# Where the FFN norms' outputs begin in SBUF, relative to the weight tiles, modulo 256 bytes

## The chip, the cores and the metric

The kernel runs on one core of a Trainium2 chip. The metric is the device time of one execution in microseconds (us); lower is better. The times shown are medians over runs of the same program.

## What is computed

Two networks in a row over 256 tokens of width 1024, all in fp32. The first has two layers of FFN, three mixers side by side (SSD, mLSTM, RWKV) and a second FFN; the second takes 256 more context tokens in and has two layers of modulated FFN, a mixer (Fourier, then retention) and another FFN. What matters here are the eight FFNs:

```python
def swiglu(x, w_gate_up, w_down):
    gate, up = jnp.split(x @ w_gate_up, 2, axis=-1)
    return (jax.nn.silu(gate) * up) @ w_down
x = x + FFN_HALF * swiglu(rms_norm(x, ffn1_norm[l]), ffn1_w_gate_up[l], ffn1_w_down[l])   # width 1024 -> 2816 -> 1024
```

In the second network the norm's output is also scaled and shifted by a modulation vector, and the result is gated.

## The kernel before

**Precision.** Every large product of `a` and `b` is made of three fp32r matmuls: `a` is split into `hi` (a cast to fp32r) and `lo` (the rest), `b` likewise, and `mm3` issues hi x hi, hi x lo and lo x hi. All of them go through `mm` on line 102. ScalarE casts a weight tile (`split_hi`, L314), VectorE subtracts (`split_lo`, L320). `mm(p, o, l, r)` loads `l` into the array (stationary) and streams `r` (moving):

```python
def mm3(p, o, wh, wl, xh, xl, start, stop):
    mm(p, o, wh, xh, start, False)
    mm(p, o, wh, xl, False, False)
    return mm(p, o, wl, xh, False, stop)
```

**Stages and tiles.** The FFN stages are f10, f20, f11, f21 (first network) and half00, half02, half10, half12 (second). Five of them work on 256 tokens (the f stages and half12: narrow), three on 512 (half00, half02, half10: wide). The gate half of a stage (`Ffn.tensor`) has 22 weight tiles of 128 x 2048. Each makes 128 gate and 128 up columns: 2 x 8 x 3 = 48 matmuls, with weights stationary and the norm's output `hs` moving, 256 or 512 columns of it. That is 22 x 48 = 1056 matmuls a stage. The back half turns it round: `hf` (the SwiGLU result) is stationary, the down-projection's weights are moving, 512 columns at a time; in a narrow stage a tile is 24 matmuls, and there are 11. The mixers project in the gate half's way (`project_t`: weights stationary, `hx` moving, 256 columns, 48 matmuls a tile).

**Order.** `network` writes the order of the stages' phases out by hand; `plan` gives each weight tile one of up to eight raw buffers (`raw0` to `raw7`, and `lo` in the same place) and a slot for its `hi` part. Narrow FFN stages have three such slots, `hi0`, `hi1`, `hi2`, in turn; wide stages, and the mixers but for their first tile, have two. The first tile of a wide stage has a spare of its own. In the order of the plan `hi2` falls on 4 of the 11 back tiles of f10 and on 3 of 11 in each other narrow stage.

**Addresses.** `Map` hands out byte offsets within a partition. `raw`, `lo`, `hi0` and `hi1` all begin at 128 modulo 256 (the allocation starts at 4224), and so do `K.free` and `END`. I call that residue the class. Slices of these tiles step by 512 or 1024 bytes, so every slice keeps its tile's residue. Before the change, `STEP = 64`: the narrow stages' `hs`, `xs`, `no` and (f stages) `rot` begin 64 bytes past the class, and so does `hi2`. `hf` is in the class everywhere, `hs` of the wide stages too, and the mixers' `hx` too. `K.free` is where the stages' scratch area starts; `hi2` is its first 8192 bytes when three slots are used.

**The norm.** `Norm` writes `hs` in two parts: ScalarE the fp32r cast, VectorE the rest of it (`low`, L601). The first tile's matmuls wait for it chunk by chunk (`Norm.ready`).

Of the kernel before, what the change touches and what calls it, by code (L numbers as in the profile page):

```python
# [8 lines left out]
F32R = mybir.dt.float32r  # L9
# [12 lines left out]
ROWS = 27648  # L22
END = 229248
LINE = 128
STEP = 64
ALL = slice(None)


class Line:


    def __init__(self, sem):
        self.sem, self.n, self.at, self.counting = sem, 0, {}, True
# [120 lines left out]
class Core:  # L154


    def __init__(self, nc, A, ctx):
        self.nc, self.A, self.ctx = nc, A, ctx
        self.lines, self.stages, self.order, self.opening = {}, {}, [], {}
        m = Map(nc, (nc.sbuf_base + LINE - 1) // LINE * LINE)  # L160
        at = [m.at + 8192 * i for i in range(5)] + [END - 8192 * (2 + i) for i in range(RAW - 5)]
        m.at = at[4] + 8192
        self.raw = [Map(nc, at[i]).take(f"raw{i}", 2048) for i in range(RAW)]
        self.far = at[3]
        self.lo = [Map(nc, at[i]).take(f"lo{i}", 2048, dt=F32R) for i in range(RAW)]
        self.hi = [m.take(f"hi{i}", 2048, dt=F32R) for i in range(2)]
        self.xt = m.take("xt", 2, 1024)
        self.msk = m.take("msk", len(MASKS), 128)
        self.mask2 = m.take("mask2", 2, 128)
        self.scanm = m.take("scanm", 256)  # L170
        self.cols = m.take("cols", NCOLS)
        self.rows = m.take("rows", 120)
        self.mods = m.take("mods", 2, 72, 2)
        self.gcol = m.take("gcol", 3, 2, 8)
        self.growt = m.take("grow", 128)
        self.st = m.take("st", 512)
        self.silb = m.take("silb", 2, 1024)
        self.prod = m.take("prod", 1024)
        m.at = (m.at + LINE) // 256 * 256 + LINE
        self.free, self.end = m.at, END  # L180
        self.hi.append(Map(nc, m.at + STEP).take("hi2", 2048, dt=F32R))
        self.ps = [ctx.enter_context(nc.psum_tensor(f"ps{i}", [P, 512], F32)) for i in range(8)]
        (self.ident, self.tri, self.ones, self.negT, self.neg, self.bones, self.l2,
         self.l2t) = (self.msk[:, i, :] for i in range(8))
        self.lvl = [self.msk[:, 8 + i, :] for i in range(5)]
        self.i2 = self.msk[:, 13, 0:64]
        self.onesrow = self.msk[0:1, 2, :]
        c2 = 2 * NCOL1
        self.ng2 = self.cols[:, c2:c2 + 48].rearrange("p (l j c) -> p l j c", l=2, j=3)
        self.ab2 = self.cols[:, c2 + 48:c2 + 192].rearrange("p (l c) -> p l c", l=2)  # L190
        self.heads = self.cols[:, c2 + 192:c2 + 224].rearrange("p (c h) -> p c h", h=8)
        self.sct = self.st[:, 256:272].rearrange("p (c v) -> p c v", v=2)
        self.xa = [self.xt[:, t, :] for t in range(2)]
        self.ring = [Loads(self.sem(f"ring{i}")) for i in range(RAW)]
        self.wac, self.wdv = Part(self.line("w", "hi"), 0), Part(self.line("w", "lo"), 0)
# [495 lines left out]
class Half:  # L691


    gates = None
# [2197 lines left out]
def network(K):  # L2892

    A, order, stages = K.A, K.order, K.stages
    filled, rows_of = [0], []

    def put(name, stage):
        stages[name], stage.key = stage, name
        return stage
# [48 lines left out]

    def first(l, which, before, since=()):
        name, gain = f"f{which}{l}", "n1" if which == 1 else "n2"  # L2950
        norm = put(name + "n", Norm(K, name + "n", [before], K.xa, K.split(8192 + STEP, name + "hs", 8, 256),
                                    K.at(ROWS + STEP, name + "xs", 2, 1024), K.at(ROWS + 8192 + STEP, name + "no", 3, 512),
                                    lambda c, s: K.col(l, gain, c)))
        s = put(name, Ffn(K, name, norm, Half(K.xa), A[f"ffn{which}_w_gate_up"][l], A[f"ffn{which}_w_down"][l], [22], 2,
                          K.at(8192 + 16384 + STEP, name + "rot", 3, 256), K.split(ROWS + 16384, name + "hf", 22, 256)))
        s.since = since
        norm.idle = None if before is setup else (0, 15) if which == 1 else (4, 15)
        if before is setup:
            for _ in range(3):
                run(norm)  # L2960
            run(setup)
        else:
            join(before, norm)
        if (l, which) != (1, 2):
            ffn(s)
        return s
# [75 lines left out]
    def half_ffn(l, j, nt, parts, rows, before, xs, o, hs, gb, rot, fin, hf, spare, turn=None):  # L3042

        name, N = f"half{l}{j}", 128 * nt
        gb = K.at(gb, name + "gb", nt // 2, 1024)
        hs = [Map(K.nc, K.free + at).take(f"{name}hs{i}", 8, N, dt=F32R) for i, at in enumerate(hs)]
        hf = [Map(K.nc, K.free + at).take(f"{name}hf{i}", max(parts), N, dt=F32R) for i, at in enumerate(hf)]
        norm = put(name + "n", Norm(K, name + "n", [before], rows[:nt], hs, K.at(xs, name + "xs", nt, 1024),
                                    K.at(o, name + "no", 3, 512), lambda c, v: K.sct[:, c, v:v + 1],
                                    lambda c, v: K.mods[:, l, 24 * j + c, v:v + 1], (l, j), turn))  # L3050
        if j == 0:
            rows_of.append(put(f"grow{l}", GateRows(K, l, norm, 6)))
        gates = put(name + "g", Gates(K, name + "g", [norm], rows_of[l], j, nt // 2, gb))
        s = put(name, Ffn(K, name, norm, Gated(gates, rows, K.at(fin, name + "fin", 2, 512)), A["ffn_gu_2"][l, j // 2],
                          A["ffn_w_down_2"][l, j // 2], parts, nt, K.at(rot, name + "rot", 3, N), hf))
        if spare:
            s.spare = Map(K.nc, K.free + spare).take(name + "hi", 2048, dt=F32R)
        return norm, [rows_of[l]] * (0 if j else 2) + [gates], s
# [6 lines left out]
    both = K.xa + [ct[:, t, :] for t in range(2)]  # L3065
    s = setup
    for l in range(2):
        s = first(l, 1, s)
        s = first(l, 2, *mixers(l, s))

    rows1 = put("rows1", RowNorm(K, "rows1", [s], K.at(89088, "fn", 1024), K.at(ROWS, "junk1", 2, 1024), A["final_norm"],
                                 None, ct))
    s.loads = [rows1]
    norm, gates, half = half_ffn(0, 0, 4, [11, 11], both, rows1, ROWS, ROWS + 16384, (0, 72704), 16384, 93184, 89088,
                                 (ROWS, 50176), 16384, [2, 3, 0, 1])
    norm.idle = 0, 30
    ffn(s, [norm, norm], late=8)
    fill_to(36)
# [3 lines left out]
    gb, rot = K.at(49152, "four_gb", 2, 1024), K.at(59392, "four_fin", 2, 512)  # L3082
    gates = put("fourgates", Gates(K, "fourg", [half], rows_of[0], 1, 2, gb))
    four = put("four", Fourier(K, "four", half, 0, both, Gated(gates, both, rot)))
    for s in (half, half, four, half, half, four, gates, four, four, four, four, four, four):
        run(s)
    for _ in range(3):
        run(four)

    norm, gates, half = half_ffn(0, 2, 4, [11, 11], both, four, 0, 16384, (45056, 61440), 90112, 77824, 83968, (0, 22528),  # L3090
                                 90112)
    norm.idle = 0, 17
    join(four, norm)
# [2 lines left out]
    before = half  # L3096
    norm, gates, half = half_ffn(1, 0, 4, [11, 11], both, before, 45056, 61440, (0, 16384), 90112, 32768, 38912,
                                 (45056, 67584), 69632)
# [4 lines left out]
    yT, hs = K.at(8192, "retyT", 16, 256), K.split(24576, "reths", 8, 512)  # L3103
    m = Map(K.nc, K.free + 57344)
    norm = put("retn", Norm(K, "retn", [half], both, hs, K.at(8192, "retxs", 4, 1024), K.at(57344, "retno", 3, 512),
                            lambda c, v: K.sct[:, c, v:v + 1], lambda c, v: K.mods[:, 1, 24 + c, v:v + 1], (1, 1)))
# [4 lines left out]
    gb, rot = K.at(57344, "retgb", 1, 1024), K.at(63488, "retfin", 2, 512)  # L3111
    gates = put("retgates", Gates(K, "retg", [ret], rows_of[1], 1, 1, gb))
    rout = put("retout", Out(K, "retout", [ret], A["ret_w_out_2"][0], yT, ys, Gated(gates, K.xa, rot), 6))
# [4 lines left out]
    for q in range(rout.phases - rout.tail):  # L3118
        run(rout)
        if q < 1:  # L3120
            run(gates)

    norm, gates, half = half_ffn(1, 2, 2, [22], K.xa, rout, 8192 + STEP, 16384 + STEP, (53504 + STEP, 61696 + STEP), 69952,
                                 79872, 75776, (8192 + 256, 30720 + 256),
                                 None)
    half.since = [ret]
    norm.idle = 0, 21
    join(rout, norm)
    ffn(half, gates)
    K.final = put("rows2", RowNorm(K, "rows2", [half], K.at(83968, "fg", 1024), K.at(53504, "junk2", 2, 1024), A["final_g_2"],  # L3130
                                   K.out))
    half.loads = [K.final]
    for _ in range(half.tail):
# [167 lines left out]
```

How the kernel before makes its waits and increments, by code:

```python
    def wait_ge(self, sem, n):  # L84
        if n > self.seen.get(sem.name, 0):
            self.seen[sem.name] = n
            if not self.counting:
                self.eng.wait_ge(sem, n)
# [1 line left out]
    def __call__(self):  # L90
        if self.chained and self.before:
            self.wait_ge(*self.before)
        return self.eng
# [213 lines left out]
    def split_hi(self, a, w):  # L307
        s, n, r, width, _ = self.weights[w]
        before = self.hislot[w][1]
        a.wait_ge(*self.landed(r))
        if before is not None:
            a.wait_ge(*self.released(*self.weights[before][0:2]))
        a().activation(self.high(w), self.raw[self.place(r)][:, 0:width], ACT.Copy).then_inc(*a.mark(self.wac, w))
# [1 line left out]
    def split_lo(self, v, w):  # L316
        s, n, r, width, _ = self.weights[w]
        v.wait_ge(*self.wac[w])
        v().tensor_tensor(self.low(w), self.raw[self.place(r)][:, 0:width], self.high(w).bitcast(F32),
                          ALU.subtract).then_inc(*v.mark(self.wdv, w))
# [1 line left out]
    def fetch(self, sp):  # L323
        for src, width, s, _, i, _, before in self.tiles:
            if i >= s.near:
                s.opened(sp)
            if before is not None:
                sp.wait_ge(*self.released(*self.tiles[before][2:4]))
            dst = self.raw[i][:, 0:width]
            if len(src.shape) == 3:
                dst = dst.rearrange("p (c n) -> p c n", n=src.shape[2])
            sp().dma_start(dst, src, max_dma_last_dim=16384).then_inc(*self.ring[i].mark())
# [70 lines left out]
    def row(self, e, t, h):  # L404
        e.wait_ge(*self.x.all)
```

## Time and profile before

| | |
|---|---|
| median of 3 runs | 3314.3 us (3309.09 to 3314.7) |
| profiled execution, its own time | 3311.61 us |
| its span, first to last instruction | 3309.7 us |
| mean granted TensorE clock | 0.989 |
| TensorE busy | 3196.1 us (97%), 19162 matmuls |
| VectorE / ScalarE / GpSimd busy | 2015.0 / 1302.9 / 115.9 us |
| DMA moved | 469.30 MB, mean 142 GB/s |

The span is what the sums are made against; 1.9 us lie around it. A line of a group gives the engine, the operation, output and inputs by name (buffer numbers left out, so `hi` stands for all three slots), the shape, the count, and the mean duration of one. Durations of matmuls overlap. A line of the timeline begins with the start of an instruction, or of the first of several.

### The profile page before, as it was taken

How to read it: one execution, taken by the hardware profiler on the slowest of the kernel's cores; microseconds unless marked ns; L12 is line 12 of the kernel's file. 1: busy time of each engine (PE TensorE's matmuls, PEld its weight loads, DVE VectorE, ACT ScalarE, POOL GpSimd, SP SyncE). 2: the span in 40 equal slices, each digit the busy share in tenths (PEclk: the TensorE clock that was granted, in tenths of full speed). 3: DMA queues.
4: the chain of work that ended last, by engine and by line, in shares of the span. 5: the costliest groups of instructions: out<-in, count | busy, mean ns of one | idle time of the engine just before them, and what ended most of it. 6: DMA issues, size and time to landing. Idle time of an engine off the chain costs nothing.

```text
span 3309.7 us, 46055 instructions
## 1 busy us (share of the span) xinstructions
PE 3196.1 (97%) x19162; PEld 2792.5 (84%) x19162; DVE 2015.0 (61%) x2437; ACT 1302.9 (39%) x1566; POOL 115.9 (4%) x126
## 2 busy tenths in 40 slices
PE   7998999999999899999999999999999999999998
PEld 7988887898989888798888877888888888887897
DVE  5777557778786657678765745744343334444554
ACT  5444244544445234554422233222242233434443
POOL 0001200000000210000000000000000000000000
PEclk9999999999999999999999999999999999999999
DMA  6652021466663012457454521543222222332552
GB/s 237 241 208 77 28 100 64 191 242 229 255 240 111 28 63 76 172 212 282 161 179 140 186 98 51 198 139 102 96 98 87 102 96 77 124 102 102 197 188 93
DMA packets 84970, 469.30 MB, mean 142 GB/s; under 512 B 7717, under 2 KB 11525, under 8 KB 44058
## 3 DMA queue, kind: packets, MB, share of 16 engines
q1 hardware_dynamic: 77952, 451.44, 37.3%
q10 hardware_dynamic: 6810, 14.91, 1.3%
q8 instruction: 151, 2.47, 0.3%
q14 instruction: 57, 0.47, 0.0%
HBM read 465.23 MB, written 1.10 MB: 141 GB/s over the span
## 4 chain that ended last, share of the span: by engine, by line
PE 77%; DVE 14%; ACT 5%; issue 1%; DMA 1%; POOL 0%; DVEq 0%; ACTq 0%; SPq 0%; POOLq 0%
PE ps L102 76%; DVE lo L320 4%; ACT hi L314 2%; DVE prod L464 1%; PE ps L522 1%; DMA raw<-in_ffn_w_gate_up 0%; DVE m1restMs L1973 0%; DVE m0restMs L1973 0%; DVE xt L685 0%; DVE ct L685 0%; DMA raw<-in_ffn_gu 0%; DVE half00fin L683 0%; DMA raw<-in_ffn_w_down 0%; DVE f21rot L855 0%; ACT f21hf_h L833 0%
## 5 line engine op out<-in xcount | busy, mean ns | idle before, releaser
L320 DVE TENSOR_TENSOR lo<-raw,hi 128x2048 fp32r<-128x2048 f32 (+1 forms) x357 | 809.6, 2268 | 604.4 <-ACT hi L314 588.9
L314 ACT ACTIVATE hi<-raw 128x2048 fp32r<-128x2048 f32 (+1 forms) x357 | 677.6, 1898 | 594.0 <-PE ps L102 469.3
L464 DVE SCALAR_TENSOR_TENSOR prod<-raw,silb 128x1024 f32<-128x1024 f32 x288 | 352.8, 1225 | 16.8 <-ACT silb L450 1.6
L102 PE MATMUL ps<-half00hs,hi 128*128 128x512 f32 x672 | 207.4, 390 | 1.0 <-DVE lo L320 1.0
L102 PE MATMUL ps<-half10hs,hi 128*128 128x512 f32 x672 | 207.2, 390 | 1.0 <-DVE lo L320 1.0
L102 PE MATMUL ps<-half02hs,hi 128*128 128x512 f32 x672 | 207.1, 389 | 1.0 <-DVE lo L320 1.0
L102 PEld LDWEIGHTS ps<-half00hs,hi 128*128 128x128 f32 x672 | 125.9, 188 | 28.4 <-DVE lo L320 2.2
L102 PEld LDWEIGHTS ps<-half02hs,hi 128*128 128x128 f32 x672 | 126.0, 188 | 27.9 <-DVE lo L320 1.9
L102 PEld LDWEIGHTS ps<-half10hs,hi 128*128 128x128 f32 x672 | 125.9, 188 | 28.0 <-DVE lo L320 1.9
L102 PE MATMUL ps<-half10hs,lo 128*128 128x512 f32 x352 | 137.2, 390 | 0.0
L102 PE MATMUL ps<-half00hs,lo 128*128 128x512 f32 x352 | 137.1, 390 | 0.0
L102 PE MATMUL ps<-half02hs,lo 128*128 128x512 f32 x352 | 137.0, 389 | 0.0
L102 PE MATMUL ps<-half12hs,hi 128*128 128x256 f32 x704 | 125.1, 280 | 2.1 <-DVE half12hs L601 2.1
L102 PEld LDWEIGHTS ps<-half12hs,hi 128*128 128x128 f32 x704 | 107.4, 188 | 3.0 <-DVE half12hs L601 1.8
L102 PE MATMUL ps<-hi,half02hf 128*128 128x512 f32 x352 | 108.8, 389 | 0.0
L102 PE MATMUL ps<-hi,half10hf 128*128 128x512 f32 x352 | 108.7, 389 | 0.0
L102 PE MATMUL ps<-hi,half00hf 128*128 128x512 f32 x352 | 108.7, 389 | 0.0
L102 PE MATMUL ps<-msk 128*128 128x128 f32 x886 | 104.5, 276 | 1.0 <-PE ps L2785 1.0
L102 PEld LDWEIGHTS ps<-msk 128*128 128x128 f32 x886 | 102.4, 192 | 3.3 <-PE ps L2785 1.2
L102 PE MATMUL ps<-f10hs_h,hi 128*128 128x256 f32 x352 | 100.0, 284 | 2.2 <-DVE lo L320 1.9
L102 PE MATMUL ps<-f11hs_h,hi 128*128 128x256 f32 x352 | 98.8, 281 | 1.7 <-DVE f11hs_l L601 1.6
L102 PE MATMUL ps<-f21hs_h,hi 128*128 128x256 f32 x352 | 98.8, 281 | 1.7 <-DVE f21hs_l L601 1.6
(898 smaller groups left out, 7767.0 us busy)
## 6 DMA issues: line engine op xcount, KB each, us to landing
raw<-in_ffn_w_gate_up SPq DMA_DIRECT2D x88, 1024.0 KB, 8.4
raw<-in_ffn_gu SPq DMA_DIRECT2D x88, 1024.0 KB, 4.9
raw<-in_ffn_w_down SPq DMA_DIRECT2D x85, 1024.0 KB, 5.0
raw<-in_ada_w SPq DMA_DIRECT2D x72, 1024.0 KB, 6.5
raw<-in_w_in_t SPq DMA_DIRECT2D x28, 1024.0 KB, 4.9
raw<-in_ret_w_in SPq DMA_DIRECT2D x24, 1024.0 KB, 4.8
raw<-in_w_out SPq DMA_DIRECT2D x16, 1024.0 KB, 4.9
raw<-in_w_in_n SPq DMA_DIRECT2D x12, 1024.0 KB, 4.9
```

The costliest lines, as they stand in the source:

```text
L102: return p().matmul(o, l, r, start=start, stop=stop, skip_group_check=True)
L314: a().activation(self.high(w), self.raw[self.place(r)][:, 0:width], ACT.Copy).then_inc(*a.mark(self.wac, w))
L320: v().tensor_tensor(self.low(w), self.raw[self.place(r)][:, 0:width], self.high(w).bitcast(F32), ALU.subtract).then_inc(*v.mark(self.wdv, w))
L464: v().scalar_tensor_tensor(out=K.prod, in0=w[:, m, :], scalar=1.0, in1=K.silb[:, n, :], op0=ALU.mult, op1=ALU.mult, accum_out=K.mods[:, l, ...
L522: x = p().transpose(b[:, t * 128:(t + 1) * 128], self.xs[:, 2 * s + t, c * 128:(c + 1) * 128], K.ident)
```

## The change

`STEP` goes. Every `hs` gets a distance of its own from the class: 32 (f10), 96 (f20), 160 (f11), 224 (f21), 192 (half12), 32 (half00), 224 (half02), 0 (half10, as before). `hi2`, `xs`, `no` and `rot` of the narrow stages go to the class itself. Neighbouring tensors move by 256 bytes where they have to make room. Instructions, their order, their waits and their sizes stay.

```diff
-STEP = 64
+BEGINS = {"f10": 32, "f20": 96, "f11": 160, "f21": 224, "half12": 192, "half00": 32, "half02": 224, "half10": 0}
...
-        self.hi.append(Map(nc, m.at + STEP).take("hi2", 2048, dt=F32R))
+        self.hi.append(Map(nc, m.at).take("hi2", 2048, dt=F32R))
...
-        norm = put(name + "n", Norm(K, name + "n", [before], K.xa, K.split(8192 + STEP, name + "hs", 8, 256),
-                                    K.at(ROWS + STEP, name + "xs", 2, 1024), K.at(ROWS + 8192 + STEP, name + "no", 3, 512),
+        norm = put(name + "n", Norm(K, name + "n", [before], K.xa, K.split(8192 + BEGINS[name], name + "hs", 8, 256),
+                                    K.at(ROWS + 256, name + "xs", 2, 1024), K.at(ROWS + 8192 + 256, name + "no", 3, 512),
...
-                          K.at(8192 + 16384 + STEP, name + "rot", 3, 256), K.split(ROWS + 16384, name + "hf", 22, 256)))
+                          K.at(8192 + 16384 + 256, name + "rot", 3, 256), K.split(ROWS + 16384, name + "hf", 22, 256)))
...
-        hs = [Map(K.nc, K.free + at).take(f"{name}hs{i}", 8, N, dt=F32R) for i, at in enumerate(hs)]
+        hs = [Map(K.nc, K.free + at + BEGINS[name]).take(f"{name}hs{i}", 8, N, dt=F32R) for i, at in enumerate(hs)]
...
-    rows1 = put("rows1", RowNorm(K, "rows1", [s], K.at(89088, "fn", 1024), K.at(ROWS, "junk1", 2, 1024), A["final_norm"],
+    rows1 = put("rows1", RowNorm(K, "rows1", [s], K.at(89344, "fn", 1024), K.at(ROWS, "junk1", 2, 1024), A["final_norm"],
...
-    norm, gates, half = half_ffn(0, 0, 4, [11, 11], both, rows1, ROWS, ROWS + 16384, (0, 72704), 16384, 93184, 89088,
-                                 (ROWS, 50176), 16384, [2, 3, 0, 1])
+    norm, gates, half = half_ffn(0, 0, 4, [11, 11], both, rows1, ROWS, ROWS + 16384, (0, 72704), 16640, 93440, 89344,
+                                 (ROWS, 50176), 16640, [2, 3, 0, 1])
...
-    norm, gates, half = half_ffn(0, 2, 4, [11, 11], both, four, 0, 16384, (45056, 61440), 90112, 77824, 83968, (0, 22528),
+    norm, gates, half = half_ffn(0, 2, 4, [11, 11], both, four, 0, 16384, (45056, 61440), 90112, 78080, 84224, (0, 22528),
...
-    norm, gates, half = half_ffn(1, 2, 2, [22], K.xa, rout, 8192 + STEP, 16384 + STEP, (53504 + STEP, 61696 + STEP), 69952,
-                                 79872, 75776, (8192 + 256, 30720 + 256),
+    norm, gates, half = half_ffn(1, 2, 2, [22], K.xa, rout, 8192, 16384, (53248, 61440), 69632 + 256,
+                                 79872, 75776, (8192, 30720),
...
-    K.final = put("rows2", RowNorm(K, "rows2", [half], K.at(83968, "fg", 1024), K.at(53504, "junk2", 2, 1024), A["final_g_2"],
+    K.final = put("rows2", RowNorm(K, "rows2", [half], K.at(83968, "fg", 1024), K.at(53248, "junk2", 2, 1024), A["final_g_2"],
```

## Rows read from the trace of the kernel before

**Rows 1.** The page's engines (busy us, share, instructions) and clock by slice.
```profile
PE 3196.1 (97%) x19162; PEld 2792.5 (84%) x19162; DVE 2015.0 (61%) x2437; ACT 1302.9 (39%) x1566; POOL 115.9 (4%) x126
...
PEclk9999999999999999999999999999999999999999
```

**Rows 2.** The page's chain that ended last, share by engine.
```profile
PE 77%; DVE 14%; ACT 5%; issue 1%; DMA 1%; POOL 0%; DVEq 0%; ACTq 0%; SPq 0%; POOLq 0%
```

**Rows 3.** The page's costliest groups: busy us, mean ns, idle before.
```profile
L102 PE MATMUL ps<-half00hs,hi 128*128 128x512 f32 x672 | 207.4, 390 | 1.0 <-DVE lo L320 1.0
...
L102 PE MATMUL ps<-half12hs,hi 128*128 128x256 f32 x704 | 125.1, 280 | 2.1 <-DVE half12hs L601 2.1
...
L102 PE MATMUL ps<-f21hs_h,hi 128*128 128x256 f32 x352 | 98.8, 281 | 1.7 <-DVE f21hs_l L601 1.6
```

**Rows 4.** Timeline, f21's gate half: tiles 3, 4, 5 and the back's start.
```profile
1398.34 0.28 PE L102 MATMUL ps<-f21hs_h,hi 128*128 128x256 f32 x1
...
1403.99 0.28 PE L102 MATMUL ps<-f21hs_h,hi 128*128 128x256 f32 x1
...
1409.64 0.28 PE L102 MATMUL ps<-f21hs_h,hi 128*128 128x256 f32 x1
...
1511.42 0.40 PE L102 MATMUL ps<-hi,f21hf_h 128*128 128x512 f32 x1
```

**Rows 5.** Busy time by stretch (counts include instructions already running at its start).
```profile
core 0: us, PE busy (x) PEld busy (x) DVE busy (x) ACT busy (x) POOL busy (x), PEclk, DMA share, GB/s
1398.34:1511.42 113.08, 113.08 (x963) 113.08 (x961) 87.66 (x102) 56.39 (x69) 1.10 (x2) 1.00 0.52 207
```

**Rows 6.** Timeline, first mixer's projection, 192 matmuls from the first to the second.
```profile
236.51 0.28 PE L102 MATMUL ps<-m0hx_h,hi 128*128 128x256 f32 x1
...
259.55 0.28 PE L102 MATMUL ps<-m0hx_h,hi 128*128 128x256 f32 x1
```

**Rows 7.** Timeline, second mixer's first tile (`hi` in `hi2`), 27 matmuls apart.
```profile
996.62 0.28 PE L102 MATMUL ps<-m1hx_h,lo 128*128 128x256 f32 x1
...
999.80 0.28 PE L102 MATMUL ps<-m1hx_h,lo 128*128 128x256 f32 x1
```

**Rows 8.** Timeline, half00's gate half, from a tile's start to the back's, 336 matmuls.
```profile
1633.10 0.39 PE L102 MATMUL ps<-half00hs,hi 128*128 128x512 f32 x1
...
1709.26 0.39 PE L102 MATMUL ps<-hi,half00hf 128*128 128x512 f32 x1
```

**Rows 9.** Timeline, f21's back half: starts of tiles in slots 0, 2, 1, 0, 2.
```profile
1516.91 0.39 PE L102 MATMUL ps<-hi,f21hf_h 128*128 128x512 f32 x1
...
1522.35 0.40 PE L102 MATMUL ps<-hi,f21hf_h 128*128 128x512 f32 x1
...
1527.94 0.40 PE L102 MATMUL ps<-hi,f21hf_h 128*128 128x512 f32 x1
...
1533.42 0.39 PE L102 MATMUL ps<-hi,f21hf_h 128*128 128x512 f32 x1
...
1538.86 0.40 PE L102 MATMUL ps<-hi,f21hf_h 128*128 128x512 f32 x1
```

**Rows 10.** Timeline: 24-column matmuls, ten apart; 17 plain-fp32 matmuls merged, and their group.
```profile
411.80 0.26 PE L102 MATMUL ps<-lo,m0hx_h 128*128 128x24 f32 x1
...
412.92 0.26 PE L102 MATMUL ps<-hi,m0hx_l 128*128 128x24 f32 x1
...
1964.30 3.83 PE L102 MATMUL ps<-fd,fZ 128*128 128x256 f32 x17
...
L102 PE MATMUL ps<-fd,fZ 128*128 128x256 f32 x64 | 14.1, 379 | 0.0
```

**Rows 11.** Line 601: duration min/median/max in ns, first and last start.
```profile
L601 DVE TENSOR_TENSOR m1hx_l<-mn1no,m1hx_h x4: 692/692/692, 991.7 to 995.5; 128x512 fp32r<-128x512 f32 x4
L601 DVE TENSOR_TENSOR f21hs_l<-f21no,f21hs_h x4: 693/693/694, 1384.3 to 1388.2; 128x512 fp32r<-128x512 f32 x4
```

**Rows 12.** TensorE's waits: total us, times, longest.
```profile
PE ps L102 <- DVE lo L320: 13.9, 15, 2.0
```

## The prediction

> **What bounds the kernel now.** I read the page's table of engines and its slices first. TensorE is busy for 97% of the span at full granted clock [rows 1], and the chain of work that ended last is 77% TensorE [rows 2]. No other engine and no queue is as near. Then the page's costliest groups: the matmuls of the gate-and-up halves of the FFN stages, all issued through `mm` on line 102 [rows 3]. The reader is to see there that two shapes carry the time, 512 columns in the wide stages and 256 in the narrow ones, and that the durations in these rows (389 and 280 ns) say nothing of the rate, since consecutive matmuls overlap. The rate is the distance between the starts of neighbours, which only the timeline shows. I call it the pitch below.
>
> The pitch is therefore what I read next, in long stretches without a wait. In the gate half of f21, 20 tiles of 48 matmuls take 1511.42 - 1398.34 = 113.08 us [rows 4], so 113.08 / 960 = 117.8 ns. TensorE and its weight loads are busy for all of that stretch at clock 1.00, VectorE for 87.66 us of it, and the DMA share is 0.52 [rows 5]: the supply of weights is not the limit there. TensorE waits for `lo` tiles 13.9 us in 15 places over the whole program [rows 12], which is nothing beside 3300.
>
> So the change can only act through the pitch. It moves no instruction, adds none and waits for nothing new. What it moves are addresses: in the gate halves the moving operand (`hs`, the norm's output) gets another distance from the weights, taken modulo 256 bytes. The question is what the trace of before says of pitch against that distance. It has both distance 0 and distance 64, and for two widths.
>
> - 256 columns, `hs` 64 bytes past the weights' class: 117.8 ns [rows 4].
> - 256 columns, everything in one class (the mixer's projection): 192 matmuls take 259.55 - 236.51 = 23.04 us, 120.0 ns [rows 6].
> - 256 columns, `hx` in the class, but `hi` weights 64 bytes past it, in slot `hi2` (the first tile of the second mixer, which may use three slots): 27 intervals take 999.80 - 996.62 = 3.18 us, 117.8 ns [rows 7]. Here the moving operand is 64 bytes before the weights, which is 192 modulo 256.
> - 512 columns, everything in one class: 7 tiles of 48 take 1709.26 - 1633.10 = 76.16 us, 226.7 ns [rows 8].
> - 512 columns in the back half of f21, where the weights are now the moving side (hf is stationary, in the class): a tile of 24 matmuls takes 5.44 us when its `hi` lies in slot 0, and 5.59 us when it lies in `hi2`, 64 bytes past the class; the tile after `hi2` takes 5.48 us [rows 9]. So 226.7 ns against 5.59 / 24 = 232.9 ns.
>
> A distance other than 0 thus gave 2.2 ns back at 256 columns and cost 6.2 ns at 512. The floors lie lower: matmuls of 24 columns, which only the weight load can hold up, start (412.92 - 411.80) / 10 = 112 ns apart, and 512 column passes of plain fp32 (fd, 256 columns at two passes each) are (3.83 - 0.38) / 16 = 215.6 ns apart [rows 10].
>
> [...] The same shape at the same clock has two pitches, 120.0 [rows 6] and 117.8 ns [rows 4], and their only difference that I find is the address. [...]
>
> **Part by part.**
>
> *Slot `hi2` goes from 64 to 0.* In the back halves of the five narrow stages its tiles become like the others. Each now costs (5.59 - 5.44) + (5.48 - 5.44) = 0.19 us more than a tile in another slot [rows 9]. The three slots take turns, so I find 4 such tiles of 11 in f10 and 3 of 11 in each of the other four: 16 x 0.19 = 3.0 us saved, all of it on TensorE's path. This is the part I trust most, since hf does not move. In the gate halves, tiles with `hi2` (equal class with `hs` today) are not distinguishable from the others: the first tile of the stretch (slot 0, from 1398.34), the second (`hi2`, from 1403.99) and the mean of all 20 are each 5.65 us [rows 4]. I cost that at 0.
>
> *Narrow gate halves, 1056 matmuls each, so 1 ns of pitch is 1.06 us.* half12 gets 192: the row nearest to it is that of 64 bytes before the weights, 117.8 ns [rows 7], so 0. f20 (96) and f11 (160) have no row; the nearest is 117.8, so 0. f10 (32) and f21 (224, which is 32 before) lie halfway between the two seen distances; I take the middle of 120.0 and 117.8, so +1.1 ns, +1.2 us each, 2.3 together. Bounds for each stage: below, the floor of 112 ns, -5.8 ns or -6.1 us; above, at least 120.0 (+2.3 us), and, if the 6.2 ns of the 512-column row came here, 124 ns (+6.5 us).
>
> *Wide gate halves of half00 (32) and half02 (224), 1056 matmuls each.* Seen: 226.7 at 0 and 232.9 at 64. Halfway is +3.1 ns, 3.3 us each, 6.6 together. Bounds for each: 215.6 ns below (-11.1 ns, -11.7 us), 232.9 above (+6.5 us). half10 stays at 0: no change, and it serves as the control.
>
> *Why I do not expect the floor.* A weight load of 128 columns takes about 112 ns [rows 10], as long as 256 columns of the moving side. The weights are 512 bytes per partition and the moving tile 1024, so in one load the two reads slide past each other by 512 bytes, twice around a circle of 256. The starting distance should then mostly wash out; what is left would be whether consecutive matmuls fall into step. That is my reasoning, not something a row shows.
>
> *The rest.* xs, no and rot of the narrow stages go from 64 to 0. VectorE's last step of the norm takes 692 ns where its operands lie in the class and 693 where they lie 64 past it [rows 11], so the norm's own work costs nothing extra; its first tiles wait for it as before. Gate rows, the final gains and `junk2` move to free space with the same class and sizes, and no DMA changes its queue or order. Casts and splits run beside TensorE with a quarter of VectorE idle in the stage [rows 5].
>
> Sum: -3.0 + 2.3 + 6.6 = +5.9 us. Against the profiled execution's 3311.6 (span 3309.7 and 1.9 around it) that is 3317.5. That execution lies 2.7 below the median of the runs shown, inside their spread, so for the median I say 3314.3 + 5.9 = 3320.
>
> **Rivals.**
>
> - *A: only equality matters.* At 256 columns, 64 ahead and 64 behind give the same 117.8 [rows 4, 7], which speaks for a mere equal/unequal switch; the wide gate halves, where one operand never changes class, might keep 226.7, since in the back tile with `hi2` the moving side alternates between 64 and 0 and the alternation may be the cost. Then only the slots' 3.0 us come: 3311. Chance 0.20.
> - *Placement has no effect*: the 2.2 and 6.2 ns come from something else in those stages, nothing moves: 3314. [...] Chance 0.04.
> - *B: the wide stages lose their step entirely.* The place is the two wide gate halves, the price that of the `hi2` tile, 6.2 ns x 2112 = 13.1 us; with +2.3 and -3.0 that is +12.4: 3327. It decides for slower once the wide pitch rises by (6.6 + 3.0) / 2112 = 4.5 ns on average, with nothing else. For it: the unequal 512-column row is the only one there is. Against it: 32 bytes is half of what that row has. Chance 0.22.
> - *C, on the other side: some distances are nearly free of conflict.* If f20 and f11, farthest from the class, reached the 112 ns floor, that is 2 x -6.1 = -12.2, with the slots -15.2: 3299. It decides for faster once the narrow pitch falls by (6.6 - 3.0) / 5280 = 0.7 ns on average. For it: moving from 0 to 64 already gave 2.2 ns, and 5.8 more lie above the floor. Against it: the sliding argument. Chance 0.20. [...]
>
> **Numbers.** The forecast case has 0.34. A measurement of this kernel tells about 0.2%, 6.6 us, from no change. The forecast lies at +5.9, just inside that line, so I give 0.18 of its chance to the same and 0.16 to slower. Of A I give 0.03 to faster, for narrow stages that fall by a few tenths of a ns as well. Slower is then 0.22 + 0.16 = 0.38, same 0.18 + 0.17 + 0.04 = 0.39, faster 0.20 + 0.03 = 0.23. The range reaches to C's 3299 and somewhat beyond B's 3327 for narrow stages that lose too: 3300 to 3333. The forecast case alone: 3314 to 3325.
>
> **What would show it.** Back halves of the narrow stages: every tile 5.44 us, no 5.59. Gate tiles of 5.65 us in half12, f20 and f11, 5.71 in f10 and f21. Wide gate tiles of 11.03 us in half00 and half02 against 10.88 today, and 10.88 in half10. Any gate tile of the narrow stages under 5.6 us proves C; 11.18 in the wide ones proves B; 10.88 there proves A. The prediction is wrong if pitch depends on distance in another way than a straight line between 0 and 64, which is its weakest step.

## The result

The median rose from 3311.70 us (4 runs, 3308.61 to 3314.70) to 3323.39 us (4 runs, 3320.70 to 3328.53). The ratio is 1.0036, with a 95% interval of 1.0021 to 1.0052, so the kernel is slower by about 12 us (7 to 17), 0.4%. The forecast was +5.9 us, 3320 on the median of 3314.3 that stood then; rival B's sum was +12.4. In the absolute number part of the miss is hidden by luck: a fourth run of before moved its median from 3314.3 to 3311.7. The profiled execution took 3328.53 us, its span is 3326.6.

### The profile after

TensorE is as full as in [rows 1]. It is busy 15.9 us longer, with the same 19162 matmuls:

```profile
PE 3212.0 (97%) x19162; PEld 2794.2 (84%) x19162; DVE 2015.3 (61%) x2437; ACT 1300.0 (39%) x1566; POOL 116.0 (3%) x126
```

The groups that answer to [rows 3]. Their mean durations (right of the bar stand the busy time in us, then the mean of one in ns) went from 390 to 395 in half00, from 280 to 277 in half12 and from 281 to 282 in f21. They show the direction in each stage, not the rate:

```profile
L102 PE MATMUL ps<-half00hs,hi 128*128 128x512 f32 x672 | 211.4, 395 | 0.7 <-DVE lo L320 0.7
...
L102 PE MATMUL ps<-half12hs,hi 128*128 128x256 f32 x704 | 120.6, 277 | 2.1 <-DVE half12hs L601 2.1
...
L102 PE MATMUL ps<-f21hs_h,hi 128*128 128x256 f32 x352 | 99.4, 282 | 1.7 <-DVE f21hs_l L601 1.6
```

The rate is in the timeline. These are the starts of two neighbouring tiles (48 matmuls apart) in the gate halves of f20, f11, f21 and half12, then of half00; they answer to [rows 4] and [rows 8]:

```profile
640.43 0.28 PE L102 MATMUL ps<-f20hs_h,hi 128*128 128x256 f32 x1
...
646.19 0.28 PE L102 MATMUL ps<-f20hs_h,hi 128*128 128x256 f32 x1
...
834.59 0.28 PE L102 MATMUL ps<-f11hs_h,hi 128*128 128x256 f32 x1
...
840.29 0.28 PE L102 MATMUL ps<-f11hs_h,hi 128*128 128x256 f32 x1
...
1425.02 0.28 PE L102 MATMUL ps<-f21hs_h,hi 128*128 128x256 f32 x1
...
1430.69 0.28 PE L102 MATMUL ps<-f21hs_h,hi 128*128 128x256 f32 x1
...
1643.90 0.39 PE L102 MATMUL ps<-half00hs,hi 128*128 128x512 f32 x1
...
1655.10 0.39 PE L102 MATMUL ps<-half00hs,hi 128*128 128x512 f32 x1
...
3165.26 0.39 PE L102 MATMUL ps<-half12hs,hi 128*128 128x256 f32 x2
...
3170.70 0.39 PE L102 MATMUL ps<-half12hs,hi 128*128 128x256 f32 x2
```

The reader is to see four different steps where [rows 4] had one: 5.76 us in f20, 5.70 in f11, 5.68 in f21, 5.44 in half12. The wide tile takes 11.20 us; it was 10.88 in [rows 8] (76.16 / 7). Every steady tile of half02 takes 11.20 too, and every one of half10, which was not moved, 10.88.

In the back half of f21 the steady tiles now all take 5.44 us, where [rows 9] had 5.59 and 5.48 around slot `hi2`:

```profile
1527.04 0.39 PE L102 MATMUL ps<-hi,f21hf_h 128*128 128x512 f32 x1
...
1532.48 0.39 PE L102 MATMUL ps<-hi,f21hf_h 128*128 128x512 f32 x1
...
1537.92 0.39 PE L102 MATMUL ps<-hi,f21hf_h 128*128 128x512 f32 x1
```

TensorE's waits for `lo` are what [rows 12] had, 15.0 us against 13.9:

```profile
PE ps L102 <- DVE lo L320: 15.0, 16, 2.5
```

Then busy time by stretch, first before and then after: from f10's last gate matmul to f20's first (this holds the first mixer), then half00 and half12 from their first to their last gate matmul (columns as in [rows 5]). Half00 works in two parts, so its stretch also holds the back half of the first part: 1322 matmuls, of which 1056 are the gate half's.

```profile
147.76:606.93 459.17, 429.28 (x3079) 383.29 (x3077) 312.40 (x438) 198.55 (x285) 47.58 (x42) 0.98 0.32 115
1588.44:1890.18 301.74, 300.71 (x1322) 248.00 (x1321) 211.63 (x264) 83.12 (x78) 0.00 (x0) 1.00 0.48 167
...
3113.67:3240.10 126.43, 125.24 (x1055) 124.60 (x1056) 73.36 (x70) 63.99 (x70) 0.00 (x0) 1.00 0.53 184
```

```profile
146.00:609.89 463.89, 433.80 (x3078) 387.01 (x3077) 313.18 (x438) 198.10 (x285) 47.63 (x42) 0.97 0.32 114
1598.38:1906.39 308.01, 307.26 (x1322) 247.11 (x1322) 211.71 (x265) 83.07 (x78) 0.00 (x0) 1.00 0.49 164
...
3135.70:3257.63 121.93, 120.75 (x1056) 120.12 (x1056) 73.13 (x70) 63.98 (x70) 0.00 (x0) 1.00 0.55 191
```

Half00 lost 6.3 us and half12 gained 4.5. Cut in this way at the first and last gate matmul of every stage, the spans of the two profiled executions compare as follows (us, after minus before):

| stretch | difference |
|---|---|
| half00 / half02, first to last gate matmul | +6.3 / +6.5 |
| gate halves of f10, f20, f11, f21 | -1.5, +2.2, +0.9, +0.5 |
| half12 / half10, first to last gate matmul | -4.5 / +0.1 |
| the stretches between the gate halves (backs, norms), without the two next | -2.2 |
| the stretches that hold the two mixers of the first network | +4.7, +4.2 |
| all, with -0.3 ahead of f10 | +16.9 |

The +4.7 and +4.2 go with TensorE's clock: in each of these two stretches the trace of after has 30.7 us at a granted clock of 0.5, that of before 20.5. Whether the change has a part in that is taken up with e11 and e12 below. Without the two stretches +8.0 is left. The medians differ by 11.7.

### The profile page after: what moved, and what is told of

Its sections match the earlier page's. It is cut to its first block, busy times and chain, and to the rows that moved or that the text cites. A ratio compares the mean times of both kernels' runs of the same rounds, so it can differ in the third digit from the quotient of the medians.

```text
span 3326.6 us, 46055 instructions
## 1 busy us (share of the span) xinstructions
PE 3212.0 (97%) x19162; PEld 2794.2 (84%) x19162; DVE 2015.3 (61%) x2437; ACT 1300.0 (39%) x1566; POOL 116.0 (3%) x126
## 4 chain that ended last, share of the span: by engine, by line
PE 75%; DVE 14%; ACT 7%; DMA 2%; issue 1%; POOL 0%; ACTq 0%; DVEq 0%; SPq 0%; POOLq 0%
PE ps L102 74%; DVE lo L320 4%; ACT hi L314 3%; DVE prod L464 1%; DMA raw<-in_ffn_w_down 1%; DMA raw<-in_ffn_w_gate_up 1%; PE ps L522 1%; DVE m0restMs L1973 0%; DVE m1restMs L1973 0%; DVE ct L685 0%; DVE xt L685 0%; DMA raw<-in_ffn_gu 0%; DVE half00fin L683 0%; DVE f10rot L855 0%; ACT f10hf_h L833 0%
## 5 line engine op out<-in xcount | busy, mean ns | idle before, releaser
L102 PE MATMUL ps<-f20hs_h,hi 128*128 128x256 f32 x352 | 100.0, 284 | 1.7 <-DVE f20hs_l L601 1.5
```

The lines of the kernel that those rows point to most:

```text
L102: return p().matmul(o, l, r, start=start, stop=stop, skip_group_check=True)
```

## The experiments

"Distance" is that of `hs` past the class, modulo 256 bytes. A tile is a gate tile of 48 matmuls unless said otherwise; its time is the steady distance between starts. All kernels compute the whole reference.

**e1: other distances.** Stages and distances are dealt out anew, and two neighbouring tensors of half10 move by 256 bytes to make room (not shown); the rest is the change's.

```diff
-BEGINS = {"f10": 32, "f20": 96, "f11": 160, "f21": 224, "half12": 192, "half00": 32, "half02": 224, "half10": 0}
+BEGINS = {"f10": 192, "f20": 128, "f11": 192, "f21": 64, "half12": 32, "half00": 192, "half02": 128, "half10": 64}
```

> The distances are dealt out anew: f10 192, f20 128, f11 192, f21 64, half12 32, half00 192, half02 128, half10 64. Theory D (the pitch is set by the distance alone): gate tiles of 5.44 us in f10 and f11 (as half12 had at 192), 5.65 in f21 (64, as before), 5.60 or 5.65 in half12 (32, as f10 had), and half10 leaves its 10.88 us for about 11.2 (233 ns, the back tiles' price at 64). Rival S (the gain belongs to the stage half12): half12 stays at 5.44, f10 and f11 stay above 5.6. For f20 at 128 and the wide stages at 192 and 128 there is no row: if 192 saves the same number of ns per matmul at 512 columns as at 256 (6.7 against distance 0), half00 has tiles of 10.56 us; 128 lies between 96 (5.76) and 160 (5.70), so 5.7 by a straight line.

One run, 3332.46 us. The narrow tiles: f20 5.70; f11, f21 and half12 5.65; f10 5.44 for three tiles and 5.65 after a wait. The wide ones: half00 11.20, half02 11.16, half10 10.99. The last two, in the timeline:

```profile
2120.30 0.39 PE L102 MATMUL ps<-half02hs,hi 128*128 128x512 f32 x1
...
2131.45 0.40 PE L102 MATMUL ps<-half02hs,hi 128*128 128x512 f32 x1
...
2499.11 0.39 PE L102 MATMUL ps<-half10hs,hi 128*128 128x512 f32 x1
...
2510.09 0.39 PE L102 MATMUL ps<-half10hs,hi 128*128 128x512 f32 x1
```

At 512 columns, a distance of 64 costs (10.99 - 10.88) / 48 = 2.2 ns a matmul, and 128 and 192 cost more. The 10.56 us expected for half00, from what 192 had saved in half12, did not come: 11.20 is a loss. And half12's 5.44 at 192 did not come again in f11: distance alone does not set the narrow tile.

**e2: all narrow stages at 192, the wide ones at 0.**

```diff
+BEGINS = {"f10": 192, "f20": 192, "f11": 192, "f21": 192, "half12": 192, "half00": 0, "half02": 0, "half10": 0}
```

> All five narrow gate halves at 192, the wide ones at 0, the slot hi2 in the class. Theory D: every narrow gate tile from the third on 5.44 us instead of the 5.65 of before, so 5 x 20 x 0.214 = 21.4 us, and 3.0 from the back halves: 24.4 us less, 3287 against 3312 of the kernel before, ratio 0.993. Rival S: only half12 gains, 4.3 + 3.0 = 7.3 us, ratio 0.998.

Ratio 0.9995 (0.9986 to 1.0004), median 3309.61 against 3311.15. f11 and half12 ran at 5.44, f10 too but for waits, and f20 and f21 at 5.65. So the 24 us of theory D did not come: by stretches the gate halves gave 11.7 us (4.5 each in f11 and half12, 2.6 in f10), and in this execution the stretches with the two mixers took 3.1 and 5.2 us more than before's.

**e5: e2 again**, unchanged.

> The kernel of e2_all192 once more, another execution. There f11 and half12 ran their gate tiles in 5.44 us and f20 and f21 theirs in 5.65, all four at distance 192. If a stage's tile time is chosen anew in each execution (two steady rhythms at one distance, picked by where the stage restarts): at least one of the four trades its value. If it belongs to the stage or its buffers: the same four values again.

One run, 3303.21 us. This time f20 ran at 5.44 as well. First f20 in e2, then f20 in e5, the same program:

```profile
637.41 0.28 PE L102 MATMUL ps<-f20hs_h,hi 128*128 128x256 f32 x1
...
643.06 0.28 PE L102 MATMUL ps<-f20hs_h,hi 128*128 128x256 f32 x1
```

```profile
631.55 0.28 PE L102 MATMUL ps<-f20hs_h,hi 128*128 128x256 f32 x1
...
636.99 0.28 PE L102 MATMUL ps<-f20hs_h,hi 128*128 128x256 f32 x1
...
1442.18 0.28 PE L102 MATMUL ps<-f21hs_h,hi 128*128 128x256 f32 x1
...
1448.24 0.38 PE L102 MATMUL ps<-f21hs_h,hi 128*128 128x256 f32 x1 [0.46 <-DVE lo L320]
...
1459.24 0.28 PE L102 MATMUL ps<-f21hs_h,hi 128*128 128x256 f32 x1
...
1465.52 0.39 PE L102 MATMUL ps<-f21hs_h,hi 128*128 128x256 f32 x1 [0.67 <-DVE lo L320]
1471.28 0.28 PE L102 MATMUL ps<-f21hs_h,hi 128*128 128x256 f32 x1
...
1476.93 0.28 PE L102 MATMUL ps<-f21hs_h,hi 128*128 128x256 f32 x1
```

So one distance has two steady rhythms (two pitches that keep up for many tiles), 5.65 and 5.44, and a stage gets one or the other. f21 shows the second thing: at 5.44 TensorE outruns its weights, waits 0.46 and 0.67 us for `lo`, and after the second wait goes on at 5.65. Not every wait does that: the first of these two did not, nor did those of 1.10, 0.30, 0.40 and 0.55 us in f10. And part of the gain goes back: f11's gate half is 4.5 us shorter than before's, but the first ten tiles of its back half take 56.34 us, with waits for `lo` of up to 0.89 us, against 54.43 in e7. The waits for `lo` over the whole program rise from the 13.9 us of [rows 12] to 22.7:

```profile
PE ps L102 <- DVE lo L320: 22.7, 28, 3.1
```

**e3: only the wide stages moved**; everything narrow as before the change. The neighbours of half00 and half02 make room as in the change (not shown).

```diff
+WIDE = {"half00": 32, "half02": 224}
...
+        hs = [Map(K.nc, K.free + at + WIDE.get(name, 0)).take(f"{name}hs{i}", 8, N, dt=F32R) for i, at in enumerate(hs)]
```

> The kernel before with only half00 at 32 and half02 at 224. If the two wide gate halves are the cause of the loss: tiles of 11.20 us instead of 10.88, 2 x 22 x 0.32 = +14.1 us, ratio 1.0043, all narrow tiles as before (5.65, and 5.59 in the back). Rival (the loss comes mostly from clock windows that fell otherwise in the mixers): under +6 us, ratio below 1.002.

Ratio 1.0042 (1.0027 to 1.0056), median 3324.21. That is the whole loss. From first to last gate matmul half00 and half02 take 308.0 us each, as in the changed kernel. The narrow stages, whose instructions and addresses are those of before, did not repeat [rows 4]: tiles went 5.44, 5.44, 5.65 in turn, with the 5.65 where `hi` is in `hi2` (f20 here), until in f21 a wait brought 5.65 for all:

```profile
637.43 0.28 PE L103 MATMUL ps<-f20hs_h,hi 128*128 128x256 f32 x1
...
642.87 0.28 PE L103 MATMUL ps<-f20hs_h,hi 128*128 128x256 f32 x1
...
648.53 0.28 PE L103 MATMUL ps<-f20hs_h,hi 128*128 128x256 f32 x1
...
1465.24 0.28 PE L103 MATMUL ps<-f21hs_h,hi 128*128 128x256 f32 x1
...
1471.08 0.39 PE L103 MATMUL ps<-f21hs_h,hi 128*128 128x256 f32 x1 [0.24 <-DVE lo L321]
...
1482.49 0.28 PE L103 MATMUL ps<-f21hs_h,hi 128*128 128x256 f32 x1
...
1488.14 0.28 PE L103 MATMUL ps<-f21hs_h,hi 128*128 128x256 f32 x1
```

The slower tile in `hi2` is no second rhythm. Its `hi` lies 64 bytes past the class, as `hs` does, so two matmuls of three are at distance 0 and the third, with `lo`, is at 64. Over the 48 matmuls of the tile from 642.87 the next start comes after 119 and 121 ns behind the two with `hi` and after 113 ns behind the one with `lo`; in the 5.44 tiles before it all three are at 64 and take 113 or 114 ns. So each matmul paid by its own distance here: 120 ns on average at 0, 113.3 at 64. One group of three:

```profile
642.87 0.28 PE L103 MATMUL ps<-f20hs_h,hi 128*128 128x256 f32 x1
642.99 0.28 PE L103 MATMUL ps<-f20hs_l,hi 128*128 128x256 f32 x1
643.11 0.28 PE L103 MATMUL ps<-f20hs_h,lo 128*128 128x256 f32 x1
643.23 0.28 PE L103 MATMUL ps<-f20hs_h,hi 128*128 128x256 f32 x1
```

This matters for every comparison with before. At the narrow addresses of before, e3 took 9.0 us less in the gate halves of f20, f11, f21 and half12 than the profiled execution of before did (2.6, 2.6, 1.2 and 2.6). They do not show in its time, since the stretches with the two mixers took 2.3 and 5.2 us more. Before was profiled once only, so what its narrow stages take in its other runs is not known.

**e9: only the narrow stages and `hi2` moved**, the counterpart of e3.

```diff
+BEGINS = {"f10": 32, "f20": 96, "f11": 160, "f21": 224, "half12": 192, "half00": 0, "half02": 0, "half10": 0}
```

> The changed kernel with half00 and half02 back at 0, its narrow distances (32, 96, 160, 224, 192) and the slot in the class kept. If the wide stages are the whole loss: 14 us less than the changed kernel, so 3309 to 3312 beside a before of 3312, ratio 0.9985 to 1.0000. Rival (the narrow distances cost too, or the mixers' clock windows do): ratio 1.001 or more.

Ratio 0.9996 (0.9983 to 1.0010), median 3310.85. The wide tiles are back at 10.88:

```profile
1645.02 0.39 PE L102 MATMUL ps<-half00hs,hi 128*128 128x512 f32 x1
...
1655.90 0.39 PE L102 MATMUL ps<-half00hs,hi 128*128 128x512 f32 x1
```

**e4: the whole change, every address 64 bytes on.** The distances stay, the absolute addresses change.

```diff
-END = 229248
+END = 229248 + 64
...
-        m = Map(nc, (nc.sbuf_base + LINE - 1) // LINE * LINE)
+        m = Map(nc, (nc.sbuf_base + LINE - 1) // LINE * LINE + 64)
...
-        m.at = (m.at + LINE) // 256 * 256 + LINE
+        m.at = (m.at - 64 + LINE) // 256 * 256 + LINE + 64
```

> The changed kernel with every address of the program 64 bytes higher, so that all distances stay. If distance between moving operand and weights is what counts: the same tiles in each stage to 0.01 us (f20 5.76, f11 5.70, f21 5.68, half12 5.44, half00 11.20, half10 10.88). Rival (the absolute address of the moving operand counts): the values trade places, half12 (absolute residue 64 further) no longer 5.44, half10 no longer 10.88.

One run, 3324.14 us. Tiles of 5.76 in f20, 5.68 in f21, 5.44 in half12, 11.20 in half00 and half02, 10.88 in half10: all as after. f11 alone has 5.63 instead of 5.70. So for a shift of 64 bytes it is the distance that counts, not the address. That it counts modulo 256 fits too: 128 is not like 0 (5.70 against 5.76, 11.16 against 10.88), and half12 and f21 of e7, whose `hs` lie 177 x 256 bytes apart at the same residue, both run at 5.65.

**e11: the changed kernel again**, unchanged.

> The changed kernel once more, another execution. Fixed by the distances in every execution, if they set the rhythm: f20 5.76, f21 5.68, half00 and half02 11.20, half10 10.88 us a tile, back tiles 5.44. Free to differ between executions: f10 (5.60 or 5.65), f11 (5.70 or 5.63), half12 (5.44 or 5.65), and the time that the two mixers take, 4 us each more in the profiled execution of the changed kernel than in that of the kernel before. If that mixer time belongs to the change, it is there again (over 192 us from the end of the projection to f20's gate half, with the same halved-clock stretches); if not, about 200 us in that stretch give way to the value of before.

3325.32 us beside 3310.31 for before. f20, f21, the wide stages and half12 repeat. f11, 5.70 in the first execution, now runs at 5.63: e4's one deviation was a second rhythm of distance 160 and not the shift. f10 (32) has two as well, 5.60 and 5.65. It changes from the slower to the faster behind a start that came 0.2 us late, 0.32 us after its neighbour instead of 0.12:

```profile
61.21 0.28 PE L102 MATMUL ps<-f10hs_h,lo 128*128 128x256 f32 x1
61.53 0.38 PE L102 MATMUL ps<-f10hs_h,hi 128*128 128x256 f32 x1
```

The extra time with the mixers is there again too: 463.24 and 462.53 us, where after had 463.89 and 463.48, and before 459.17 and 459.30. By the test set for this run that speaks for the change as their cause; e9 and e12 (below) speak against it.

**e6: what was missing of the eight distances.** Room in half10 as in e1.

```diff
+BEGINS = {"f10": 128, "f20": 64, "f11": 64, "f21": 160, "half12": 64, "half00": 96, "half02": 160, "half10": 192}
```

> Distances not yet seen with all weights in the class: narrow f10 128, f20 64, f11 64, f21 160, half12 64; wide half00 96, half02 160, half10 192. If two rhythms exist at 64 as at 192: each of f20, f11 and half12 is either at 5.44 or at 5.65 us throughout, nothing between. half10 at 192 gives 11.20 us as half00 did at 192. half00 at 96 and half02 at 160: nothing below 10.88 if equality is the best case at 512 columns; a tile under 10.88 would make moving the wide stages worth while.

One run, 3324.43 us. Wide tiles of 11.20 (96), 11.25 (160) and 11.20 (192). Narrow ones of 5.70 (f10 and f21), 5.65 (f20 and f11 at 64), and 5.44 in half12, also at 64.

**e8: the two parts of `hs` at different distances**, (hi, lo): f10 (0, 192), f20 (192, 0), f11 (64, 192), f21 (192, 128), half12 (192, 64). The wide stages are at 0. The places where `placed` is called are left out.

```diff
+SPLIT = {"f10": (0, 192), "f20": (192, 0), "f11": (64, 192), "f21": (192, 128), "half12": (192, 64)}
...
+        return [Map(K.nc, K.free + at + d).take(f"{name}hs_{n}", 8, 256, dt=F32R) for n, at, d in (("h", a, h), ("l", b, l))]
...
```

> The two parts of the norm's output get different distances (high part, low part): f10 0, 192; f20 192, 0; f11 64, 192; f21 192, 128; half12 192, 64. Wide stages at 0. If each matmul is slowed by its own distance and the others' do not count: f20 lies two thirds of the way to 192, between 5.44 and 5.65 us, and f10 between 5.65 and 5.76. If a change of residue from one matmul to the next has a price of its own: f20, f21 and f10 above 5.76. f11 and half12 mix the two distances that have a 5.44 rhythm: 5.44 or 5.65 if the rhythm survives the mixing.

One run, 3314.49 us: 5.65 in every narrow stage but f21, 5.71 there. No stage found 5.44.

**e7: only the slot.** The kernel before, with `hi2` in the class.

```diff
-        self.hi.append(Map(nc, m.at + STEP).take("hi2", 2048, dt=F32R))
+        self.hi.append(Map(nc, m.at).take("hi2", 2048, dt=F32R))
```

> The kernel before with only the slot hi2 moved from 64 to the class. Back halves of the narrow stages: every tile 5.44 us, none of 5.59, 3.0 us less. Forecast of the prediction: gate halves unchanged at 5.65, ratio 0.999. Theory of the two rhythms: with no slot that differs, each narrow gate half stays in the rhythm it falls into, 5.44 or 5.65, so between 3 and 24 us less, ratio 0.993 to 0.999.

Ratio 0.9997 (0.9987 to 1.0006), median 3310.82. Every steady gate tile of the narrow stages takes 5.65. The back tiles of f20, f11, f21 and half12 take 5.44, 0.6 us less per stage. f10's back half gains only 0.1: two of its tiles take 6.04 and 5.57 us, beside a wait for `lo` of 0.44. The 3.0 us forecast are inside the interval; the median cannot show them, the tiles show 2.4 of them.

**e12: e7 again**, unchanged.

> The kernel of e7_slot_only (all narrow stages at 64, all weights in the class) once more. There all five gate halves ran at 5.65 us a tile, while at 192 most ran at 5.44. If the choice between the two rhythms at 64 is open in each execution as it is at 192: one or more stages at 5.44 this time. If 64 leads to the slow one from nearly every restart: 5.65 in at least four of five.

3316.46 us, 6.9 us above e7's profiled 3309.53, with the same steady tiles in the FFN stages. Most of it, 4.3 us, lies in the stretch with the first mixer, in e7 and then in e12:

```profile
146.12:604.01 457.89, 426.27 (x3078) 380.15 (x3077) 312.99 (x438) 198.02 (x285) 47.55 (x42) 0.99 0.32 116
```

```profile
147.74:609.95 462.21, 432.18 (x3078) 385.80 (x3077) 312.54 (x438) 198.07 (x285) 47.63 (x42) 0.97 0.31 114
```

The same instructions took 4.3 us more at a granted clock of 0.97 than at 0.99: the trace of e7 has 13.7 us at half clock in that stretch, that of e12 27.3. So a spread of this size needs no change of address. e9, which has the changed kernel's addresses in everything that runs up to half00, took 458.2 there, with 17.1 us at half clock. But of the four executions with exactly these addresses it is the only one that did: after took 463.89, e4 464.0 and e11 463.24, the three longest of all fourteen. Over whole runs the granted clock does not tell the two kernels apart (0.988 to 0.990 in the four runs of the changed one, 0.983 to 0.990 in 47 of before). Whether the change makes the slow stretches likelier is open.

**e10: e2, and the mixers' `hx` at 192 too.** It moves `hx`, and three small tensors ahead of it, 64 bytes before the class.

```diff
+        m.at -= 64
...
+        m.at += 64
```

> e2_all192 with the mixers' hx at 192 as well (they were at 0 and took 5.76 us a tile). Where hx is the moving side, 256 columns: 5.44 or 5.65 us a tile, 28 tiles, so 3 to 9 us less. Where it is stationary under 512 columns of moving weights (distance 64): 240 matmuls a mixer at 229 to 233 ns instead of 227, 1 to 3 us more. Together ratio 0.997 to 0.9995 against the kernel before.

Ratio 0.9986 (0.9976 to 0.9996), median 3309.09 against 3312.83: the only kernel whose interval lies below 1. It overlaps with that of e2 (0.9986 to 1.0004), so what the mixers' `hx` adds is not shown by the time. The first mixer's projection tiles fall from 5.76 to between 5.53 and 5.73.

The steady tiles of all runs by distance, with all weights in the class but where e3 is named (us; ns per matmul in brackets). At 512 columns 64, 96, 128 and 160 were seen in one stage of one execution each, so a second rhythm there is not ruled out.

| distance | 256 columns | 512 columns |
|---|---|---|
| 0 | 5.76 (120.0), mixers | 10.88 (226.7) |
| 32 | 5.60 (116.7) or 5.65 | 11.20 (233.3) |
| 64 | 5.65 (117.8); 5.44 (113.3) in one stage of 14, and in e3 | 10.99 (228.9) |
| 96 | 5.76 (120.0) | 11.20 (233.3) |
| 128 | 5.70 (118.7) | 11.16 (232.4) |
| 160 | 5.70 (118.7) or 5.63 (117.3) | 11.25 (234.3) |
| 192 | 5.44 (113.3) or 5.65 (117.8) | 11.20 (233.3) |
| 224 | 5.68 (118.3) | 11.20 (233.3) |

## Why the prediction was off in size, step by step

**The bound** held. The loss came through TensorE's pitch, and the distance modulo 256 is what moves it: e4 shifts every address and repeats the pitches, but for f11's second rhythm. (The 389 ns that the prediction reads from [rows 3] stand there as 390; nothing rests on it.) The rival that placement has no effect is out: at a granted clock of 1.00 the same shape runs at pitches from 113.3 ns (half12 of after, 3165.26 to 3170.70) to 120.0 ns (f20 of after, 640.43 to 646.19).

**Slot `hi2`, -3.0 us:** the price of a tile was right, the sum 0.9 us too high. Over the first ten back tiles (nine in f21) f20, f11, f21 and half12 are 0.6 us shorter each, which is three tiles at 0.19. The 0.8 us of f10's four tiles did not come: its ten tiles take 55.64 us, before 55.34, and TensorE sits idle for 0.60 us there until a `lo` tile is ready, where before has no such gap. Together -2.1.

```profile
168.94 0.50 PE L102 MATMUL ps<-hi,f10hf_h 128*128 128x512 f32 x1 [0.60 <-DVE lo L320]
```

**Wide gate halves, +6.6 us: this is the term that was mis-sized, by 6.2 us.** "Halfway is +3.1 ns" put 32 bytes on a straight line between 0 and 64. The pitch is 233.3 ns, +6.7, and by stretches the two cost 6.3 + 6.5 = +12.8. e3 alone brings the whole loss and e9 without them none. That is near rival B's 6.2 ns, and B's sign, tiles of 11.18 us, came true with 11.20; but the reason for that row was not good either. It is of a tile where only two matmuls of three are unequal and the weights are the moving side. The gate tile at the same 64 bytes costs 2.2 ns, the least of all, and 32 costs three times as much. The price rises, falls and rises again with the distance (6.7 ns at 32, 2.2 at 64, 6.7 at 96); interpolation had no basis, and with e1 and e6 all eight are seen: 0 is the best of them at 512 columns.

**Narrow gate halves, +2.3 us:** -2.4 by stretches (f10 -1.5, f20 +2.2, f11 +0.9, f21 +0.5, half12 -4.5). The sum is 4.7 us off, and would be further off if errors of the terms did not cancel in part. f20 at 96 lost 2.2 where 0 stood, half12 at 192 won 4.5 where 0 stood, and f10's -1.5 is not the change's, since e3 and e7 have it with `hs` of f10 where it was. [Rows 7] were read as 117.8 for 192, but in that tile the third matmul of each three has `lo`, at distance 0, so the row mixes 192 and 0. And 117.8 for 64 was one rhythm of two: e3 has 113.3 at the same addresses, and there the `hi2` tiles, which the prediction could not tell from the others, cost 0.21 us more. So against another execution of before this term could be up to 9 us different. Rival C, fast distances, was half right, and its sign, a narrow tile under 5.6 us, came true: 113.3 ns exists, at 192 and sometimes at 64, not at 96 and 160 where I looked for it.

**Why I did not expect the floor:** the sliding argument is refuted. The starting distance doesn't wash out, it decides between 113.3 and 120.0 ns. The floor that I took, 112 ns [rows 10], was nearly reached; the 215.6 ns for 512 columns were not: 113.3 and 226.7 are the least.

For the 112 ns the trace of before shows more than [rows 10]. With weights of 128 columns, matmuls of 1 moving column (530.04 to 530.71), of 24 (411.80 to 412.92) and of 128 (320.37 to 321.15) all start 111 to 112 ns apart, so the number of moving columns does not set it there. With weights of 64 columns and 128 moving ones they start in pairs, 109 ns from pair to pair (359.95 to 360.60), so again 128 columns of weights go in for every step. The 112 ns are the distance between the starts of two loads; each load lasts 192 ns there, so they overlap.

For plain fp32 it shows a cost, not passes: 215.6 ns between starts at 256 columns [rows 10] and 429 at 512 (`rv`, 12 matmuls from 2856.90: (5.31 - 0.59) / 11), so 0.84 ns a column, where the fp32r matmuls of [rows 8] take 226.7 / 512 = 0.44. "Two passes" is the prediction's word for this factor of 1.9.

**The sum.** Slots -2.1, wide +12.8, narrow -2.4 give +8.3; the medians of before and after differ by 11.7 (interval 7 to 17 from the ratio), those of before and e9 by -2.0, of before and e3 by 13.1. What is left of the 11.7 is smaller than what the half-clock time in the mixers' stretches (e7 and e12) or the rhythm of before's narrow stages (e3) moves in an execution, and with four runs a side it can't be told from them. The range, 3300 to 3333, held because it was drawn wide enough for B.

**Shown and open.** Shown: the distance sets the possible pitches (113.3 to 120.0 ns at 256 columns, 226.7 to 234.3 at 512); the wide stages make the loss (+13.1 us in e3, -2.0 in e9); in one rhythm of e3 each matmul pays by its own distance (120 ns at 0, 113.3 at 64); behind a wait the rhythm can be another (5.65 us a tile after 5.44 in f21 of e5). Not shown: by what the distance acts on the pitch, why some distances have two rhythms, what picks one at a restart, whether the mixers' slow stretches have to do with the change. e8 was to tell which of the two parts of `hs` matters and tells only that 5.44 did not come up with unequal parts, in one execution.

## What to carry to other kernels

When TensorE is the bound, read its pitch (starts of neighbouring matmuls) stage by stage and compare it across operand addresses modulo 256; measure each distance that will be used at each width, because the cost is no line between two seen ones. Here equality has the best pitch for 512 moving columns (226.7 ns), and 192 most often has the best for 256 (113.3); in the time of the whole program e2, which uses both, is not told from before (0.9986 to 1.0004). Before trusting a pitch, look at a second execution: it may have two (5.44 and 5.65 us a tile in f20 of e5 and e2). Before comparing two kernels, profile the old one twice as well. And a faster pitch is worth only what the supply of weights lets through (f11 in e5: 4.5 us won in the gate half, 1.9 lost in the back half).

## What the hardware showed that was not expected

- The same program at the same addresses runs a stage at 5.44 or at 5.65 us a tile (e2 and e5); the gate half of f11 in e2 takes 121.67 us, that of f20 126.12. Of 21 stages at 192 in all profiled executions 18 began at 5.44; of 14 with everything at 64 and `hi2` in the class, one did.
- Behind a wait of 0.24 or 0.67 us for `lo` the rhythm can be the slower one for the rest of the stage (f21 in e3 and e5), but a wait of 1.10 us left it as it was (f10 in e5). In e11 a start that came 0.2 us late in f10 went with a change to the faster one: 5.65 before it, 5.60 after.
- In f20, f11 and half12 of e3 the tiles alternate by the address of their weights alone (5.44, 5.44, 5.65, the last with `hi` in `hi2`), without any wait, and within the slower tile the price goes matmul by matmul: 119 and 121 ns at distance 0, 113 at 64.
- Two executions of one program differ by 4.3 us in a stretch of 460 with the granted clock, 0.99 against 0.97 on average, or 13.7 against 27.3 us of it at half clock (e7 and e12).
